# A two-layer hybrid decoder trunk: the projections behind a layer norm start on four sets of 128 columns k by k, and TensorE multiplies into an unread bank in the pause ahead of them

## The chip, the core and the metric

The kernel runs on one core of a Trainium2 chip. Its engines work in parallel, each through its own program in order, and they wait for each other through semaphores: PE (TensorE, matrix products into the eight banks of PSUM), DVE (VectorE), ACT (ScalarE), POOL (GpSimd) and SP (SyncE, which here only issues DMAs). The metric is the device time of one execution in microseconds (us).

## The reference

256 tokens and 16 learned meta tokens (272 columns in the kernel) pass through two layers. Each layer reads a normalised residual stream of 2048 features, mixes it in three ways behind one input projection, projects the result back, normalises, and applies a gated MLP of width 5632 with a causal convolution.

```python
h = _layer_norm(concatenate([meta, x], axis=1), ln_in_g, ln_in_b)
for l in range(DEPTH):                                   # DEPTH = 2
    m = _mixer(h, ...)                                   # begins with proj = h @ w_in
    h = _layer_norm(ALPHA * h + m, ln1_g[l], ln1_b[l])
    f = _conv_ffn(h, ...)
    h = _layer_norm(ALPHA * h + f, ln2_g[l], ln2_b[l])
return h[:, N_META:, :]

def _conv_ffn(h, w_up, conv_w, conv_b, w_down):
    a = h @ w_up
    ...
    val, gate = jnp.split(a, 2, axis=-1)
    return (jax.nn.silu(gate) * val) @ w_down
```

Everything is float32. There are five layer norms: n = 0 at the start, 1 and 2 in layer 0, 3 and 4 in layer 1.

## The kernel before

**Layout.** Features lie on the partitions, tokens on the free axis. `h` is the residual, 16 tiles k of 128 features by 272 tokens. A float32 product is made of three products of a shorter type (fp32r): high part of the weights times high and low part of the data, and low part of the weights times the high part of the data (L440 to L442 in `split_block`, L559 to L561 in `in_blocks`). So each tile of `h` has a high part `x_hi` and a low part `x_lo`.

**Weights.** They stream from HBM in blocks of 128 x 1024 values (512 KB) into four slots of `raw`. Of each block ACT makes the high part (`cast`, L821, into `w_hi`) and DVE the low part (`low_part`, L1154, `raw` minus `w_hi`, into `w_lo`, `in_lo_a` or `in_lo_b`). All three buffers have four slots (`SLOTS = 4`). The cast of block b waits until PE has used block b - 4 (`block_used`), and PE waits for the low part (`lo_made`, `in_lo_made`).

**A block's products.** In the up projection of the MLP a block holds 4 tiles k by 256 columns, that is two sets of 128 columns, and 24 products. Four blocks in a row (96 products) fill two banks with one group. Even groups lie in banks 0 and 1, odd ones in banks 2 and 3. In the input projection a block holds 8 tiles k by 128 columns, 24 products too; the first eight blocks are, by `IN_ORDER`, the sets 0 to 3 over k 0 to 7, and then the sets 0 to 3 over k 8 to 15, in banks 0 to 3.

**The norm.** Sums over the features are made by PE with a matrix of ones (L485 the mean, L492 the squares). Then DVE and ACT take turns. `layer_norm` on DVE: the mean's rest `shift` (L1225), its square (L1227), the variance (L1235), then `unshift` (L1231, adds `shift` to four tiles of `h`), the reciprocal of the deviation (L1241) that ACT takes the root for (L833), and a loop over eight chunks of two tiles: scaling (L1250), low part `x_lo` (L1255), with the later `unshift`s and three or four low parts of the next weights (L1154) between them at places that `late_lows` gives. `layer_norm` on ACT, for each chunk: gain and bias (L837, two instructions), then the high part `x_hi` (L842). Only behind all eight chunks does ACT go on with the cast of the fifth block (number 4).

**Behind the norms.** n = 1 and 3 stand ahead of the up projection, n = 2 (and 0) ahead of the input projection. In the up projection ACT and DVE run a loop over pairs of groups from the first group on: four casts (four low parts), then `convolve` (conv on ACT L1098 and DVE L1794, gate on ACT L1102, product on DVE L1805 to L1809). In the input projection ACT and DVE first prepare the tables of the state space: an exponential on ACT (L861), then a chain on DVE from L1446 on, with the low parts of the blocks 4 to 7 (L1154) at fixed places in it, up to `abp` (L1368), for which PE waits at its transposes (L501).

## Time and profile before

| | |
|---|---|
| time, median of 3 runs (lowest, highest) | 2651.67 us (2650.14, 2654.08) |
| the profiled execution | 2649.61 us |
| its span, first to last instruction | 2647.8 us |
| PE busy | 2529.2 us, 96% |
| DVE busy | 1784.7 us, 67% |
| ACT busy | 1370.3 us, 52% |
| TensorE's granted clock, mean | 0.979 of 2.4 GHz |

All rows name source lines as L and the number. A span of 2647.8 us with PE at 96% leaves little idle time in all; where it lies, and which engine ends it, is read from the waits and from the order in time around the norms. The five norms end near 31, 540, 1353, 1857 and 2631 us of the span.

### The profile page before, as it was taken

Reading aid. Unit: us, or ns where it says so; the run is one execution under the profiler, and the core shown is the slowest. Engines: PE = TensorE matmul, PEld = TensorE weight load, DVE = VectorE, ACT = ScalarE, POOL = GpSimd, SP = SyncE. Lnnn points to the kernel's source line nnn. Section 1 sums busy time; section 2 is a strip of 40 time slices with the busy share of each in tenths; the row PEclk is TensorE's granted clock in tenths of the full one; section 3 lists DMA queues with packets and bytes.
Section 4 is the critical chain, followed back from the end, with each engine's and each line's share of the span. In section 5 each row is a group of like instructions: output and inputs, shape, how many; then the busy total and the mean of one; then the engine's idle time right before and its main releaser. Section 6 shows DMA issues by size and latency. Waiting matters only on the chain.

```text
span 2647.8 us, 54314 instructions
## 1 busy us (share of the span) xinstructions
PE 2529.2 (96%) x21018; PEld 2414.3 (91%) x21018; DVE 1784.7 (67%) x2820; ACT 1370.3 (52%) x2131; POOL 12.2 (0%) x21
## 2 busy tenths in 40 slices
PE   5999999989999999999989999998899999999997
PEld 4999788879999999999979997888899999998886
DVE  6887577776666666545578875877766666665555
ACT  5444465465556555433354444654666556653433
POOL 0000000000000000000000000000000000000000
PEclk8999999989999999999989999999999999999998
DMA  4433232435555555555534332333455555555553
GB/s 165 152 114 129 70 113 96 136 127 169 180 173 175 168 181 173 176 172 176 174 136 158 114 132 68 112 104 128 145 181 182 183 180 177 189 183 190 184 189 114
DMA packets 109723, 401.76 MB, mean 152 GB/s; under 512 B 12176, under 2 KB 12176, under 8 KB 109584
## 3 DMA queue, kind: packets, MB, share of 16 engines
q1 hardware_dynamic: 108432, 395.15, 45.6%
q0 software_dynamic: 1152, 4.63, 0.4%
q8 instruction: 103, 1.69, 0.3%
q14 instruction: 36, 0.29, 0.0%
HBM read 397.50 MB, written 2.23 MB: 151 GB/s over the span
## 4 chain that ended last, share of the span: by engine, by line
PE 86%; DVE 9%; ACT 3%; issue 2%; DMA 1%; SPq 0%; ACTq 0%; DVEq 0%
PE ps L440 19%; PE ps L441 18%; PE ps L442 18%; PE ps L456 6%; PE ps L559 4%; PE ps L561 4%; PE ps L560 4%; PE ps L458 3%; PE ps L711 3%; PE ps L524 1%; PE ps L698 1%; DVE h L1250 1%; DVE h L1231 1%; PE ps L677 1%; PE ps L533 1%
## 5 line engine op out<-in xcount | busy, mean ns | idle before, releaser
L821 ACT ACTIVATE w_hi<-raw 128x1024 fp32r<-128x1024 f32 x728 | 764.5, 1057 | 767.4 <-PE ps L442 521.4
L1154 DVE TENSOR_TENSOR w_lo<-raw,w_hi 128x1024 fp32r<-128x1024 f32 x528 | 638.4, 1223 | 507.3 <-ACT w_hi L821 507.1
L441 PE MATMUL ps<-x_lo,w_hi 128*128 128x272 f32 (+1 forms) x2944 | 841.8, 286 | 0.0
L442 PE MATMUL ps<-x_hi,w_hi 128*128 128x272 f32 (+1 forms) x2944 | 840.4, 285 | 0.0
L440 PE MATMUL ps<-x_hi,w_lo 128*128 128x272 f32 (+1 forms) x2816 | 807.1, 287 | 20.1 <-DVE x_lo L1255 19.7
L442 PEld LDWEIGHTS ps<-x_hi,w_hi 128*128 128x128 f32 x2944 | 556.3, 189 | 0.0
L441 PEld LDWEIGHTS ps<-x_lo,w_hi 128*128 128x128 f32 x2944 | 556.3, 189 | 0.0
L440 PEld LDWEIGHTS ps<-x_hi,w_lo 128*128 128x128 f32 x2816 | 531.9, 189 | 23.2 <-issue 16.9
L561 PE MATMUL ps<-x_hi,w_hi 128*128 128x272 f32 (+1 forms) x960 | 279.7, 291 | 0.0
L560 PE MATMUL ps<-x_lo,w_hi 128*128 128x272 f32 (+1 forms) x960 | 279.6, 291 | 0.0
L456 PE MATMUL ps<-g_both,w_hi 128*128 128x512 f32 x704 | 246.4, 394 | 0.0
L440 PE MATMUL ps<-g_both,w_lo 128*128 128x272 f32 x704 | 203.3, 289 | 0.0
L441 PE MATMUL ps<-g_both,w_hi 128*128 128x272 f32 x704 | 202.5, 288 | 0.0
L442 PE MATMUL ps<-g_both,w_hi 128*128 128x272 f32 x704 | 202.1, 287 | 0.0
L458 PE MATMUL ps<-g_both,w_lo 128*128 128x256 f32 x704 | 197.1, 280 | 0.0
L560 PEld LDWEIGHTS ps<-x_lo,w_hi 128*128 128x128 f32 x960 | 185.6, 193 | 1.2
L561 PEld LDWEIGHTS ps<-x_hi,w_hi 128*128 128x128 f32 x960 | 185.5, 193 | 0.0
L559 PE MATMUL ps<-x_hi,in_lo_a 128*128 128x272 f32 (+1 forms) x480 | 149.1, 311 | 21.3 <-DVE x_lo L1255 10.8
L440 PE MATMUL ps<-y_hi,gated_w 128*128 128x272 f32 (+1 forms) x512 | 155.6, 304 | 9.2 <-DVE h L1278 7.9
L1794 DVE SCALAR_TENSOR_TENSOR conv<-ps,cpar,conv 128x271 f32<-128x271 f32 (+1 forms) x352 | 159.4, 494 | 3.1
L456 PEld LDWEIGHTS ps<-g_both,w_hi 128*128 128x128 f32 x704 | 132.3, 188 | 30.8
L442 PE MATMUL ps<-y_hi,w_hi 128*128 128x272 f32 (+1 forms) x512 | 149.1, 291 | 0.0
(287 smaller groups left out, 3827.7 us busy)
## 6 DMA issues: line engine op xcount, KB each, us to landing
raw<-stream SPq DMA_DIRECT2D x744, 512.0 KB, 3.4
h<-x SPq DMA_DIRECT2D x4, 544.0 KB, 6.3
out<-h SPq DMA_DIRECT2D x4, 544.0 KB, 2.7
cst<-consts POOLq DMA_DIRECT2D x2, 724.0 KB, 6.4
wkv<-w_kv POOLq DMA_DIRECT2D x2, 512.0 KB, 7.8
b_st<-ssm_b POOLq DMA_DIRECT2D x2, 512.0 KB, 9.2
c_st<-ssm_c POOLq DMA_DIRECT2D x2, 512.0 KB, 10.6
par<-params SPq DMA_DIRECT2D x1, 562.0 KB, 12.1
```

The costliest lines, as they stand in the source:

```text
L440: pe.matmul(acc, lo_w[:, kk, cols], hi, start=k == 0, stop=False)
L441: pe.matmul(acc, w_hi[:, slot, kk, cols], lo, start=False, stop=False)
L442: mm = pe.matmul(acc, w_hi[:, slot, kk, cols], hi, start=False, stop=k == tiles - 1)
L456: pe.matmul(ps[:, bank + j, 0:2 * n].rearrange("p (h t) -> p h t", h=2), w_hi[:, slot, kk, cols], hi_lo, start=k == 0, stop=False)
L458: mm = pe.matmul(ps[:, bank + j, 0:n], lo_w[:, kk, cols], hi_lo[:, 0, :], start=False, stop=k == tiles - 1)
L559: pe.matmul(acc, lo_w[:, kk, :], x_hi[:, k, t0:NT], start=k == 0, stop=False)
L560: pe.matmul(acc, hi_w[:, kk, :], x_lo[:, k, t0:NT], start=False, stop=False)
L561: mm = pe.matmul(acc, hi_w[:, kk, :], x_hi[:, k, t0:NT], start=False, stop=k == DT - 1)
L711: mm = pe.matmul(ps[:, 2 * (g % 2) + j, 0:NT], raw[:, n % SLOTS, kk, j * P:j * P + P], proj[:, U0 + k, :], start=k == 0, stop=k == UT - 1)
L821: act.activation(w_hi[:, slot, :, :], raw[:, slot, :, :], ACT.Copy).then_inc(hi_made, 1)
L1154: dve.tensor_tensor(w_low(phase, slot), raw[:, slot, :, :], w_hi[:, slot, :, :].bitcast(F32), ALU.subtract).then_inc(in_lo_made if phase = ...
L1794: last = dve.scalar_tensor_tensor(out=cv[:, j, tap:NT], in0=ps[:, 2 * odd + j, 0:NT - tap], scalar=cpar[:, odd, 2 + 2 * tap + j:3 + 2 * ta ...
```

## The change

1. **PE, first blocks.** `first_blocks` works through two blocks at once: for each tile k the 12 products of four sets of 128 columns. A chunk of two tiles meets 24 products in place of 12 (input projection: 6). The stream holds the first eight blocks of both projections in the order `FIRST_BLOCKS`: group 0 and 1 over k 0 to 3, group 0 and 1 over k 4 to 7, then group 0's two other blocks, then group 1's. The places are (0, 1), (2, 3), 4, 5, 6, 7; each pair waits for the low parts of both of its blocks. The loops over groups start at 1 in place of 0.
2. **PE, pause.** `idle_products` behind the sums of n = 1, 2 and 3: 10 turns of a loop of four products of a tile with itself into bank 7, which nothing reads.
3. **DVE, norm.** The first `unshift` takes two tiles in place of four, the other two come singly behind; the low part of the next block 1 stands right behind the first scaling, those of 2 and 3 further back; every `x_lo` has a place written by hand. n = 0 makes its low part 0 ahead of the reciprocal.
4. **ACT and DVE, up projection.** The first two groups stand ahead of the loop, and the first `convolve` waits for two blocks more (place 5 is the last of group 0). The input projection's first four sets are read in pairs.

```diff
+FIRST_BLOCKS = [0, 4, 1, 5, 2, 3, 6, 7]
+IDLE = 40
...
-                    it = loop.enter_context(pe.Fori(0, groups // body)) if groups > body else 0
+                    it = loop.enter_context(pe.Fori(1, groups // body)) if groups > body else 0
...
+            def first_blocks(l, phase, places, lows, t0=0):
+                sets = [(FIRST_BLOCKS[n] // KB, (first_block(l, phase) + n) % SLOTS) for n in places]
+                b = FIRST_BLOCKS[places[0]] % KB
+                pe.wait_ge(lows, first_low(l, phase) + places[-1] + 1)
+                for kk in range(KB):
+                    k = b * KB + kk
+                    if k % 2 == 0:
+                        pe.wait_ge(xlo_made, CHUNKS * (2 * l + (phase == "up")) + k // 2 + 1)
+                    for p, slot in sets:
+                        lo_w = w_low(phase, slot).rearrange("p a b -> p (a b)").rearrange("p (k m) -> p k m", k=KB)
+                        for j in range(2):
+                            acc = ps[:, 2 * p + j, t0:NT]
+                            cols = slice(j * P, j * P + P)
+                            pe.matmul(acc, lo_w[:, kk, cols], x_hi[:, k, t0:NT], start=k == 0, stop=False)
+                            pe.matmul(acc, w_hi[:, slot, kk, cols], x_lo[:, k, t0:NT], start=False, stop=False)
+                            mm = pe.matmul(acc, w_hi[:, slot, kk, cols], x_hi[:, k, t0:NT], start=False, stop=k == DT - 1)
+                        if kk == KB - 1:
+                            mm.then_inc(block_used, 1)
+            def idle_products(tile):
+                with pe.Fori(0, IDLE // 4):
+                    for _ in range(4):
+                        pe.matmul(ps[:, 7, 0:NT], tile[:, 0:P], tile, start=True, stop=True)
...
                 mm.then_inc(var_made, 1)
+                if n < 2 * DEPTH:
+                    idle_products(y_hi[:, 0, :] if n % 2 else g_hi[:, 0, :])
...
-                products(l, "up", x_parts, lambda k: (xlo_made, CHUNKS * ln + k // 2 + 1), LAST_T0[0] if l == DEPTH - 1 else 0)
+                pe.wait_ge(psum_free, first_group(l, "up") + 2)
+                for places in ((0, 1), (2, 3), (4,), (5,), (6,), (7,)):
+                    first_blocks(l, "up", places, lo_made, query_t0(l))
+                products(l, "up", x_parts, None, query_t0(l))
...
+                first = unshift(0, 1) if n else None
                 dve.wait_ge(dev_made, n + 1)
                 mark(dve.reciprocal(rstd[:, :], rstd[:, :]))
...
+                scale(0, first)
+                low_w(1)
+                if n:
+                    low_x(0)
+                    second = unshift(1, 1)
+                    scale(1, second)
+                    third = unshift(2, 2)
+                    scale(2, third)
+                    low_x(1)
+                    low_w(2)
+                    scale(3)
+                    low_x(2)
+                    fourth = unshift(4, 2)
+                    scale(4, fourth)
+                    low_w(3)
+                    low_x(3)
+                    scale(5)
+                    fifth = unshift(6, 2)
+                    low_x(4)
+                    scale(6, fifth)
+                    low_x(5)
+                    scale(7)
...
+                low_x(6)
+                low_x(7)
...
-                with act.Fori(0, FT - 2, 2) as i:
+                for e in range(2):
+                    for n in range(4):
+                        cast(l, "up", 4 * (e + 1) + n)
+                    convolve(e, e)
+                with act.Fori(2, FT - 2, 2) as i:
```

How the instructions stand on the engines. Names are those of the tiles; line numbers of the changed kernel differ.

DVE at norm n = 1, from the first `unshift` on (`h<-h,sq_out`; 128x1088 is four tiles, 128x544 two); before:

```order
L1231 TENSOR_TENSOR h<-h,sq_out 128x1088
L1241 RECIPROCAL rstd<-rstd 128x272 [waits dev_made]
L1250 TENSOR_TENSOR h<-h,rstd 128x544 [waits dve_step]
L1250 TENSOR_TENSOR h<-h,rstd 128x544
L1255 TENSOR_TENSOR x_lo<-h,x_hi 128x544 [waits xhi_made]
L1231 TENSOR_TENSOR h<-h,sq_out 128x1088
L1250 TENSOR_TENSOR h<-h,rstd 128x544 [waits dve_step]
L1154 TENSOR_TENSOR w_lo<-raw,w_hi 128x1024 [waits hi_made]
```

and in the changed kernel:

```order
L1286 TENSOR_TENSOR h<-h,sq_out 128x544
L1309 RECIPROCAL rstd<-rstd 128x272 [waits dev_made]
L1293 TENSOR_TENSOR h<-h,rstd 128x544 [waits dve_step]
L1200 TENSOR_TENSOR w_lo<-raw,w_hi 128x1024 [waits hi_made]
L1300 TENSOR_TENSOR x_lo<-h,x_hi 128x544 [waits xhi_made]
L1286 TENSOR_TENSOR h<-h,sq_out 128x544
L1293 TENSOR_TENSOR h<-h,rstd 128x544 [waits dve_step]
L1286 TENSOR_TENSOR h<-h,sq_out 128x1088
```

The shift of the second chunk is an instruction of its own now, and a weight's low part stands between the first and the second scaling.

ACT between the last high part of norm n = 1 (`x_hi<-h`) and the casts of the blocks from number 4 on (`w_hi<-raw`); before:

```order
L842 ACTIVATE x_hi<-h 128x544 [waits h_made]
L1108 UNCONDITIONAL_BRANCH
L1108 ISA
L820 REGISTER_ALU [waits w_loaded0]
L821 ACT_TABLE_LOAD
L821 ACTIVATE w_hi<-raw 128x1024 [waits block_used]
```

and in the changed kernel:

```order
L880 ACTIVATE x_hi<-h 128x544 [waits h_made]
L859 ACTIVATE w_hi<-raw 128x1024 [waits block_used,w_loaded0]
L859 ACTIVATE w_hi<-raw 128x1024 [waits block_used,w_loaded1]
L859 ACTIVATE w_hi<-raw 128x1024 [waits block_used,w_loaded2]
L859 ACTIVATE w_hi<-raw 128x1024 [waits block_used,w_loaded3]
```

The load of a table at the head of ACT's loop is gone; the changed ACT program has no table load inside that loop either, and its first one behind this place is at the first gate.

PE from the last sum of squares (`ps<-sq_out,ones_p`) to the first products of the up projection; before:

```order
L492 MATMUL ps<-sq_out,ones_p 128x272
L410 UNCONDITIONAL_BRANCH
L410 ISA
L417 ISA [waits psum_free]
L440 MATMUL ps<-x_hi,w_lo 128x272 [waits xlo_made,lo_made]
```

and in the changed kernel:

```order
L521 MATMUL ps<-sq_out,ones_p 128x272
L501 UNCONDITIONAL_BRANCH
L503 MATMUL ps<-y_hi 128x272 x4
L501 REGISTER_ALU
L501 COMPARE_AND_BRANCH
L478 MATMUL ps<-x_hi,w_lo 128x272 [waits xlo_made,lo_made,psum_free]
```

The small loop of four products stands between the sums and the wait for the first low part of the data.

## Rows read from the trace of the kernel before

**Rows 1.** Waits of PE: engine line <- releaser: total us, times, longest

```profile
PE ps L440 <- DVE x_lo L1255: 19.7, 9, 6.9
...
PE ps L501 <- DVE abp L1368: 2.9, 2, 1.5
...
PE ps L440 <- DVE w_lo L1154: 0.2, 1, 0.2
```

**Rows 2.** Timeline of PE at norm 1: start, us, instruction, idle before

```profile
546.77 0.57 PE L440 MATMUL ps<-x_hi,w_lo 128*128 128x272 f32 x1 [6.94 <-DVE x_lo L1255]
...
565.54 0.29 PE L442 MATMUL ps<-x_hi,w_hi 128*128 128x272 f32 x1
565.89 0.39 PE L440 MATMUL ps<-x_hi,w_lo 128*128 128x272 f32 x1
```

**Rows 3.** Timeline of ACT at norm 1

```profile
540.34 0.43 ACT L833 ACTIVATE rstd<-rstd 128x272 f32<-128x272 f32 x1 [5.48 <-DVE rstd L1235]
...
560.40 1.12 ACT L837 ACTIVATE h<-h,par 128x272 f32<-128x272 f32 x2 [0.59 <-DVE h L1250]
561.55 0.66 ACT L842 ACTIVATE x_hi<-h 128x544 fp32r<-128x544 f32 x1
562.22 1.28 ACT L821 ACT_TABLE_LOAD   x1
563.52 3.91 ACT L821 ACTIVATE w_hi<-raw 128x1024 fp32r<-128x1024 f32 x4
```

**Rows 4.** Timeline of DVE at norm 1

```profile
540.23 1.28 DVE L1231 TENSOR_TENSOR h<-h,sq_out 128x1088 f32<-128x1088 f32 x1
541.42 1.84 DVE L1241 RECIPROCAL rstd<-rstd 128x272 f32<-128x272 f32 x1
...
548.50 1.22 DVE L1154 TENSOR_TENSOR w_lo<-raw,w_hi 128x1024 fp32r<-128x1024 f32 x1
549.64 0.72 DVE L1250 TENSOR_TENSOR h<-h,rstd 128x544 f32<-128x544 f32 x1
550.27 0.72 DVE L1255 TENSOR_TENSOR x_lo<-h,x_hi 128x544 fp32r<-128x544 f32 x1
...
559.64 0.72 DVE L1250 TENSOR_TENSOR h<-h,rstd 128x544 f32<-128x544 f32 x1
...
564.61 4.63 DVE L1154 TENSOR_TENSOR w_lo<-raw,w_hi 128x1024 fp32r<-128x1024 f32 x4 [1.65 <-ACT w_hi L821]
```

**Rows 5.** Norm 2: last high part on ACT, head of DVE's chain, PE's wait

```profile
1373.81 0.66 ACT L842 ACTIVATE x_hi<-h 128x544 fp32r<-128x544 f32 x1
...
1376.05 0.19 DVE L1446 TENSOR_TENSOR small<-par,small 128x32 f32<-128x32 f32 x1 [0.37 <-ACT small L861]
...
1395.88 0.87 PE L501 MATMUL ps<-cst,abp 128*128 128x128 f32 x6 [1.44 <-DVE abp L1368]
```

**Rows 6.** A convolution inside the loop: its start on ACT, its last two steps on DVE

```profile
651.56 1.05 ACT L1098 ACTIVATE conv<-ps,cpar 128x272 f32<-128x272 f32 x2
...
654.99 0.44 DVE L1805 TENSOR_TENSOR prod<-gate,conv 128x272 f32<-128x272 f32 x1 [0.50 <-ACT gate L1102]
...
656.00 0.44 DVE L1809 TENSOR_TENSOR g_both<-prod,g_both 128x272 f32 x1 [0.21 <-DVE g_both L1806]
```

**Rows 7.** Stretches: us, busy (instructions) of PE, PEld, DVE, ACT, POOL, granted clock, DMA

```profile
531.50:534.20 2.70, 0.00 (x0) 0.00 (x0) 2.70 (x5) 1.06 (x1) 0.00 (x0) 1.00 0.01 3
534.20:537.60 3.40, 3.38 (x8) 2.56 (x9) 2.69 (x4) 0.66 (x1) 0.00 (x0) 0.50 0.47 154
566.00:600.00 34.00, 34.00 (x272) 34.00 (x273) 24.10 (x34) 20.91 (x28) 0.00 (x0) 1.00 0.62 198
1849.90:1853.20 3.30, 0.20 (x2) 0.00 (x0) 3.20 (x6) 1.18 (x3) 0.00 (x0) 1.00 0.00 0
1853.20:1856.60 3.40, 3.40 (x14) 2.62 (x15) 3.12 (x6) 0.64 (x1) 0.00 (x0) 1.00 0.48 154
1810.80:1817.60 6.80, 6.03 (x28) 6.03 (x29) 5.25 (x7) 0.53 (x2) 0.00 (x0) 0.50 0.55 188
```

More of the change, by code:

```diff
@@ L420, in products @@
                             else:
-                                split_block(phase, slot, b, 2 * (g % 2), blocks * KB, rhs, ready if g == 0 else None, t0)
+                                split_block(phase, slot, b, 2 * (g % 2), blocks * KB, rhs, ready if ready and g == 0 else None, t0)
                         if phase != "up" and g == 2:
@@ L1236, in layer_norm, with unshift, scale, low_x @@
                                              op0=ALU.mult, op1=ALU.subtract).then_inc(spread_made, 1)
-                    unshifted = [unshift(0)]
                 else:
                     first_norm_stats()
+                    low_part(*low_parts, 0)
+                def unshift(c, chunks):
+                    part = h[:, 2 * c:2 * (c + chunks), :]
+                    return mark(dve.tensor_tensor(part, part, spread(shift, 2 * chunks), ALU.add))
+                def scale(c, shifted=None):
+                    if shifted:
+                        after(shifted)
+                    h2 = h[:, 2 * c:2 * c + 2, :]
+                    dve.tensor_tensor(h2, h2, spread(rstd[:, :], 2), ALU.mult).then_inc(scaled, 1)
+                def low_x(c):
+                    if n < 2 * DEPTH:
+                        dve.wait_ge(xhi_made, CHUNKS * n + c + 1)
+                        t = slice(2 * c, 2 * c + 2)
+                        dve.tensor_tensor(x_lo[:, t, :], h[:, t, :], x_hi[:, t, :].bitcast(F32), ALU.subtract).then_inc(xlo_made, 1)
+                def low_w(b):
+                    if low_parts:
+                        low_part(*low_parts, b)
+                first = unshift(0, 1) if n else None
                 dve.wait_ge(dev_made, n + 1)
@@ L1242, in layer_norm @@
                 after()
-                late_lows = (1, 4, 5, 6) if n == 0 else (2, 4, 6) if n % 2 else (4, 6, 7)
-                for c in range(CHUNKS + 2):
-                    if c < CHUNKS:
-                        if n and c % 2 == 0:
-                            after(unshifted[c // 2])
-                        h2 = h[:, 2 * c:2 * c + 2, :]
-                        dve.tensor_tensor(h2, h2, spread(rstd[:, :], 2), ALU.mult).then_inc(scaled, 1)
-                    if (c == 1 or c >= 3) and n < 2 * DEPTH:
-                        part = max(c - 2, 0)
-                        dve.wait_ge(xhi_made, CHUNKS * n + part + 1)
-                        t = slice(2 * part, 2 * part + 2)
-                        dve.tensor_tensor(x_lo[:, t, :], h[:, t, :], x_hi[:, t, :].bitcast(F32),
-                                          ALU.subtract).then_inc(xlo_made, 1)
-                    if n and c in (1, 3, 5):
-                        unshifted.append(unshift(c // 2 + 1))
-                    if low_parts and c in late_lows:
-                        low_part(*low_parts, 4 - len(late_lows) + late_lows.index(c))
+                scale(0, first)
@@ new lines, in layer_norm @@
+                low_w(1)
[19 more added lines that the diff above has]
+                    scale(7)
+                else:
+                    scale(1)
+                    low_x(0)
+                    scale(2)
+                    low_x(1)
+                    low_w(2)
+                    scale(3)
+                    low_x(2)
+                    scale(4)
+                    low_w(3)
+                    low_x(3)
+                    scale(5)
+                    low_x(4)
+                    scale(6)
+                    low_x(5)
+                    scale(7)
@@ L1809, in convolve @@
                     dve.tensor_tensor(lo, pr_, hi.bitcast(F32), ALU.subtract).then_inc(g_made, 1)
-                with dve.Fori(0, FT - 2, 2) as i:
+                for e in range(2):
+                    for n in range(4):
+                        low_part(l, "up", 4 * (e + 1) + n)
+                    convolve(e, e)
+                with dve.Fori(2, FT - 2, 2) as i:
                     for e in range(2):
```

37 lines of the change are left out of this document (23 added, 14 removed).

## The prediction

> **What bounds the kernel now.** I read the waits of PE first, since PE is busy for 96% of the span. Its largest group is the wait for `x_lo` at the norms: 19.7 us in the up projections, of it 6.9 us at once [rows 1]. That looks like the prize of this change: more products for each chunk of data, and no cold start. But idle time ahead of a stage is worth something only if the wait that ends last in the stage moves. So I read the timelines in order.
>
> At norm 1 PE starts its products at 546.77 and issues the last of the first group at 565.54; the fifth block's first product follows at 565.89 [rows 2]. The wait there is only 0.2 us, for `w_lo` [rows 1], so two chains end at almost the same moment: PE's 96 products, and the fifth block's low part. The second chain is this: ACT makes the last `x_hi` at 561.55, loads a table at 562.22, casts block 4 at 563.52 [rows 3]; DVE makes its low part at 564.61 [rows 4]; PE starts 1.28 us behind that. With four slots PE can't do more than 96 products before that moment, in whatever order they come. From 566 on it is busy without a gap at the full clock, 272 products in 34.00 us [rows 7], so what is won or lost at 565.89 is carried to the end.
>
> At norm 2 the last wait is another: PE waits for `abp` at its transposes until 1395.88, 1.44 us idle, and `abp` ends DVE's chain that started at 1376.05, released by ACT behind its last `x_hi` at 1373.81 [rows 5]. Norm 0 has the same shape.
>
> So the question is not how fast PE gets through the first chunks, but when ACT's last `x_hi` is made.
>
> **The change part by part.**
>
> *The norm on DVE, n = 1.* Distances from start to start: 0.64 us for two tiles (549.64 to 550.27), 1.14 for a low part of weights (548.50 to 549.64) [rows 4]; a shift that the next instruction needs costs its full length and 0.04, so 1.32 for four tiles and 0.76 for two. The first shift of two tiles takes 0.64, and ACT's root ends at 540.77 [rows 3], so the reciprocal starts at 540.87 in place of 541.42 [rows 4]: 0.55 us early. The first scaling starts 1.84 + 0.04 later, at 542.75. From there to the last scaling the new order holds 13 steps of 0.64 (seven scalings, six `x_lo`), three low parts of 1.14, shifts of 0.76 + 1.32 + 1.32 + 1.20, and one wait of 0.82 for the first `x_hi` (0.76 + 1.15 [rows 3] + 0.69 behind the scaling, less 1.78 of work done meanwhile): 8.32 + 3.42 + 4.60 + 0.82 = 17.16, so it starts at 559.91. Before it was 559.64 [rows 4]. ACT needs 1.71 us a chunk (1.15 from gain to `x_hi` [rows 3], then 0.56, the 0.66 of the `x_hi` less its overlap with the next) and gets the last two scalings only 1.28 apart, so its last `x_hi` starts at 558.63 + 0.76 + 1.71 + 1.15 = 562.25, against 561.55: **0.70 us later**.
>
> *The table.* Before, the casts behind the norm stand at the head of a loop and a table is loaded there: 1.30 us from 562.22 to 563.52 [rows 3]. The changed program has none at this place. The cast starts 0.56 behind the `x_hi`, at 562.81, the low part 1.09 later at 563.90, PE 1.28 later at 565.18: **0.71 us earlier** than 565.89. The Trainium skill (ScalarE: Activation LUTs, What ACT_TABLE_LOAD costs) prices a change of table at 1.28 us for the load and 1.38 for a drain, 2.66 in all; the row has 1.28 and the next cast right behind it, so it shows no drain here. By the page each up projection would gain 1.4 us more, and the sum below would be 2.7 us lower.
>
> *k by k.* The first product comes at 546.24 (0.55 early). Chunk 0 gives 24 products x 0.125 = 3.0 us, to 549.2; chunk 1 has its `x_lo` at 550.1 and ends at 553.2; the second pair waits for low part 3, which DVE ends at 555.6, so chunk 2 ends at 558.8 and chunk 3 at 561.8. All 96 products are then done, and PE stands still for **3.4 us** until 565.18. The weave gains nothing: it moves the pause from ahead of the chunks to ahead of block 4.
>
> *What that pause costs.* Pauses of this length have gone both ways. Behind one of 2.7 us the granted clock was 0.50 (1.2 GHz) for the next 3.4 us; behind one of 3.3 us it stayed at 1.00; once the low stretch was 6.8 us long [rows 7]. At the low level 28 products took 6.03 us, 0.215 each, where 0.12 is usual: 0.45 us lost for each us. Here nothing hides it, since PE is the bound from block 4 on. A low stretch of 3.4 us costs 1.5 us, none costs 0, one of 6.8 costs 3.0. I take 1.5 for each up projection: the pause will be longer than 2.7 us, and at norm 3 it is 3.8 us, since the 258 columns there make PE faster.
>
> *Idle products.* 40 x 0.125 = 5.0 us behind the sums, inside a pause of 6.9 us [rows 1]. If a turn of the loop costs nothing beside its products they end 1.4 us ahead of the first chunk and keep the clock up for it. That is worth nothing, because the time at which block 4 starts doesn't hang on it. Bounds: 0, and, if the turns are slow, still 0 up to 3.4 us of delay.
>
> *First convolution.* It may start when group 0 is complete, T. With the start on ACT as 0, the product's last step comes at 4.44 (651.56 to 656.00 [rows 6]), the low part of block 8 0.36 behind it, its end 1.22 later, PE 0.06 later: 6.1, and 0.2 from T to the start. PE needs it when places 6 and 7 are done, 6.0 us behind T (5.76 at norm 3). A new wait of **0.3 and 0.5 us**.
>
> *Norm 2.* The same 17.16 us of DVE, but before, the third low part stood behind the last scaling. With the first scaling at 1356.15 the same steps put the last `x_hi` at 1375.65, against 1373.81 [rows 5]: 1.84 us later. The table for the exponential is still loaded there. The whole chain to `abp` shifts by that, and PE's wait with it: **+1.84 us**. PE itself isn't late: block 4 can start at 1382.0, and even with 6.8 us at the low clock its four blocks end at 1397.1, ahead of 1397.7.
>
> *Norms 0 and 4.* At n = 0 low part 0 goes into DVE's idle time ahead of the reciprocal; by the same steps ACT ends 0.3 us earlier. At n = 4 the reciprocal is 0.55 early, the extra shift costs 0.76: +0.2.
>
> *Sum.* -0.3 (n = 0) + (-0.71 + 0.3 + 1.5) + 1.84 + (-0.71 + 0.5 + 1.5) + 0.2 = **+4.1 us**. On the profiled execution (span 2647.8, time 2649.6) that gives 2653.7; the median of the runs is 2.06 above it, so 2651.7 + 4.1 = **2655.8 us**. Bounds of the sum: +1.1 with no fall of the clock, +7.1 with the long ones.
>
> **The rivals.**
>
> A. *The clock holds in both pauses.* For it speaks the pause of 3.3 us behind which it stayed at 1.00, against it the one of 2.7 us [rows 7]. The rest stays: +1.1, **2652.8 us**.
>
> B. *Slower: the pause ahead of block 4 brings a low stretch of 6.8 us in both up projections.* PE's work for the chunks is pressed together, then it stands still 3.4 and 3.8 us, and starts cold where it is the bound. For it speaks the stretch of 6.8 us [rows 7]. It counts as slower once the two stretches lose 4.2 us together. +1.1 + 2 x 3.0 = +7.1, **2658.8 us**. The Trainium skill (TensorE: Matmul & The Clock Gate, HAM oscillation) describes just this: groups of products shorter than the wait between them leave the engine cold for each next group. The rows agree for one pause and disagree for another.
>
> C. *Faster, as the change is meant.* If block 4 could start when the 96 products are done, 561.8 in place of 565.9, each up projection would gain 4.1 us: with -0.3, +1.84 and +0.2 that is -6.5, **2645.2 us**. Against it stand the order of casts on ACT and the four slots; it needs a chain behind the last `x_hi` that is 3.4 us shorter than I worked out.
>
> D. *The idle loop doesn't do what it says.* If a turn takes 1.4 us in place of 0.5, the loop ends at 554 and the 96 products, 12.0 us, at 566; the pause is filled with late work, the clock holds, and each up projection starts block 4 some 0.8 us later than in A: +2.7, **2654.4 us**. No row shows so short a loop on PE.
>
> **How the numbers follow.** Forecast 0.45, A 0.20, B 0.18, C 0.06, D 0.05, others 0.06 (half of them faster). The range takes in A, D, the forecast and B's centre with a run's own spread of some 2 us (2650.1 to 2654.1 before): 2650.5 to 2660. What a measurement of this kernel can tell from no change is about 0.2%, 5.3 us: slower begins at 2657.0. Slower holds B and the upper part of the forecast (one long and one short stretch, +5.6): 0.32. Faster: C and half of the others: 0.09. Within: 0.59.
>
> **What the changed profile would show.** The first product at norm 1 some 0.5 us earlier behind the sums, and a granted clock of 1.00 in the stretch of the chunks where it was 0.50. A wait of PE for `w_lo` of 3 to 4 us ahead of block 4, twice, where it was 0.2. No table load between the last `x_hi` and the cast, and PE's restart 2.93 us behind that `x_hi`'s start, in place of 4.34. At norm 2 the last `x_hi` 1.8 us later, measured from the sums of squares, and PE's wait at the transposes longer. After the restart a stretch at 0.50. I am wrong if the last `x_hi` is not later at norms 1 and 2, if PE has no pause ahead of block 4, or if a stall that these rows don't hold shows up, such as an engine slowed by PE's extra reads.

## The result, and the profile after

| | before | changed kernel |
|---|---|---|
| median of 13 runs each (lowest, highest) | 2650.14 us (2647.42, 2654.36) | 2656.69 us (2652.47, 2659.67) |
| ratio to before, 95% interval | | 1.0019 [1.0012, 1.0026] |
| the profiled execution, its span | 2649.61, 2647.8 us | 2656.88, 2655.1 us |
| PE, DVE, ACT busy | 2529.2, 1784.7, 1370.3 us | 2544.8, 1784.3, 1269.5 us |

The change costs about 0.2%, 3 to 7 us by the interval. The forecast was 2655.8, +4.1 us. Its starting point was the median of three runs, 2651.67, which lies 1.5 us above the median of 13 here.

**Waits of PE** in the changed kernel (columns as in [rows 1]):

```profile
PE ps L478 <- DVE x_lo L1300: 12.1, 7, 5.8
PE ps L478 <- DVE w_lo L1200: 9.7, 4, 3.4
```

The prize that [rows 1] seemed to offer was collected: of the 19.7 us for `x_lo` in the up projections alone, 12.1 are left over all norms, in good part because 5 us of idle products now fill each pause (25.0 without them, in experiment 1). In its place stand waits for low parts of weights, 9.7 us where there were 0.2, and the time is no better. The pause has moved from ahead of the chunks to ahead of block 4.

**ACT and DVE at norm 1**, timelines (start, us, instruction, idle before), for [rows 3] and [rows 4]:

```profile
563.95 0.66 ACT L880 ACTIVATE x_hi<-h 128x544 fp32r<-128x544 f32 x1
564.51 2.94 ACT L859 ACTIVATE w_hi<-raw 128x1024 fp32r<-128x1024 f32 x3
...
565.59 2.36 DVE L1200 TENSOR_TENSOR w_lo<-raw,w_hi 128x1024 fp32r<-128x1024 f32 x2 [0.22 <-ACT w_hi L859]
```

**PE at norm 1**, for [rows 2]: the sums' last products, the idle products, the first product of the first pair of sets, of its second chunk, of the second pair, the last of the 96, block 4.

```profile
540.70 0.85 PE L521 MATMUL ps<-sq_out,ones_p 128*128 128x272 f32 x3
541.19 5.38 PE L503 MATMUL ps<-y_hi 128*128 128x272 f32 x40
547.94 0.36 PE L478 MATMUL ps<-x_hi,w_lo 128*128 128x272 f32 x1 [1.38 <-DVE x_lo L1300]
...
551.86 0.39 PE L478 MATMUL ps<-x_hi,w_lo 128*128 128x272 f32 x1 [0.67 <-DVE x_lo L1300]
...
557.37 0.60 PE L478 MATMUL ps<-x_hi,w_lo 128*128 128x272 f32 x1 [2.22 <-DVE w_lo L1200]
557.76 0.43 PE L479 MATMUL ps<-x_lo,w_hi 128*128 128x272 f32 x1
...
564.82 0.29 PE L480 MATMUL ps<-x_hi,w_hi 128*128 128x272 f32 x1
566.87 0.39 PE L478 MATMUL ps<-x_hi,w_lo 128*128 128x272 f32 x1 [1.76 <-DVE w_lo L1200]
```

The first row merges three products of the sums, of which the last starts at 541.16. The 40 idle products take 5.4 us and end ahead of the first chunk. No table is loaded between `x_hi` and the cast, and PE restarts 2.92 us behind that `x_hi` (4.34 before). But the `x_hi` itself is later, and PE, which has worked off the 96 products at 564.82, stands still for 2 us. At norm 3 the pause is longer, and the clock behind it is low from the first product:

```profile
1884.62 0.28 PE L480 MATMUL ps<-x_hi,w_hi 128*128 128x258 f32 x1
1888.34 0.53 PE L478 MATMUL ps<-x_hi,w_lo 128*128 128x258 f32 x1 [3.44 <-DVE w_lo L1200]
1888.67 0.42 PE L479 MATMUL ps<-x_lo,w_hi 128*128 128x258 f32 x1
```

**Stretches** of the changed kernel (columns as in [rows 7]): the idle products; the first low stretch, inside the woven products; the one behind the restart at norm 1; the one behind the restart at norm 3; and the stretch that follows at norm 1.

```profile
541.20:547.90 6.70, 5.37 (x42) 5.11 (x40) 5.53 (x7) 2.21 (x4) 0.00 (x0) 1.00 0.08 12
557.30:560.70 3.40, 3.33 (x15) 3.33 (x16) 3.40 (x6) 2.47 (x5) 0.00 (x0) 0.51 0.50 158
567.50:570.90 3.40, 3.40 (x18) 3.40 (x17) 2.72 (x3) 1.00 (x2) 0.00 (x0) 0.50 0.77 234
...
1888.40:1891.80 3.40, 3.40 (x16) 3.40 (x17) 3.29 (x3) 1.56 (x3) 0.00 (x0) 0.50 0.75 201
...
571.00:605.00 34.00, 33.96 (x271) 33.73 (x270) 21.77 (x32) 16.82 (x23) 0.00 (x0) 1.00 0.57 190
```

In 3.40 us at the low level PE starts 16 and 18 products; at the full one, with 0.125 us each, it would be 27. So 9 to 11 products are missing, 1.1 to 1.4 us. Nothing is given back later: 34 us hold 272 products before [rows 7] and 271 after.

**Norm 2**, for [rows 5]: the last high part, the head of DVE's chain, PE's wait.

```profile
1378.46 0.66 ACT L880 ACTIVATE x_hi<-h 128x544 fp32r<-128x544 f32 x1
1379.14 1.28 ACT L899 ACT_TABLE_LOAD   x1
...
1380.69 0.19 DVE L1536 TENSOR_TENSOR small<-par,small 128x32 f32<-128x32 f32 x1 [0.81 <-ACT small L899]
...
1400.52 1.09 PE L532 MATMUL ps<-cst,abp 128*128 128x128 f32 x8 [1.06 <-DVE abp L1458]
```

**Distances.** Absolute times of two executions can't be compared stage by stage, because the start of a stage carries what happened ahead of it. So all timelines are read from the same place: z is the start of the last product of a norm's sums (at norm 1 539.44 before, 541.16 after; at norm 2 1352.84 and 1355.68; at norm 3 1856.93 and 1862.65). In us, one profiled execution of each kernel:

| | before | after | no idle products | norm only | loops only | table back | casts early | scalings first | both | early, no weave |
|---|---|---|---|---|---|---|---|---|---|---|
| norm 1: z to first product | 7.34 | 6.78 | 6.77 | 6.77 | 7.34 | 6.78 | 6.78 | 6.78 | 6.78 | 7.34 |
| z to last `x_hi` | 22.11 | 22.79 | 22.76 | 22.76 | 22.11 | 22.77 | 23.89 | 22.77 | 23.91 | 22.41 |
| z to last of 96 products | 26.10 | 23.66 | 22.18 | 25.71 | 26.10 | 22.19 | 23.61 | 22.19 | 22.21 | 26.64 |
| z to block 4 | 26.45 | 25.71 | 25.68 | 27.10 | 26.22 | 27.20 | 23.73 | 25.69 | 22.35 | 26.76 |
| norm 1 to norm 2 | 813.41 | 814.52 | 814.42 | 814.06 | 813.08 | 816.88 | 810.90 | 814.46 | 809.61 | 813.62 |
| norm 2: z to last `x_hi` | 20.97 | 22.78 | 22.77 | 22.76 | 20.98 | 22.77 | 22.76 | 18.92 | 18.92 | 20.98 |
| z to PE's transposes | 43.03 | 44.84 | 44.82 | 44.83 | 43.05 | 44.82 | 44.82 | 41.53 | 41.52 | 43.06 |
| norm 3: z to last of 96 | 25.94 | 21.97 | 23.44 | 25.66 | 25.94 | 23.44 | 21.98 | 23.44 | 23.44 | 26.60 |
| z to block 4 | 26.46 | 25.69 | 25.68 | 27.11 | 26.06 | 27.20 | 22.35 | 25.68 | 23.56 | 26.73 |
| norm 3 to norm 4 | 773.25 | 774.56 | 774.53 | 773.90 | 772.74 | 775.90 | 769.71 | 774.53 | 770.82 | 773.40 |

The columns behind the second are experiments 1 to 8 below, in their order. The rows "norm 1 to norm 2" and "norm 3 to norm 4" run from z to z and hold the MLP.

### The profile page after: what moved, and what is told of

Same layout as the page of the kernel before. It is cut to its first block, busy times and chain, and to the rows that moved or that the text cites. A ratio compares the mean times of both kernels' runs of the same rounds, so it can differ in the third digit from the quotient of the medians.

```text
span 2655.1 us, 54291 instructions
## 1 busy us (share of the span) xinstructions
PE 2544.8 (96%) x21138; PEld 2431.2 (92%) x21138; DVE 1784.3 (67%) x2824; ACT 1269.5 (48%) x2049; POOL 12.2 (0%) x21
## 4 chain that ended last, share of the span: by engine, by line
PE 86%; DVE 8%; ACT 3%; issue 2%; DMA 1%; SPq 0%; ACTq 0%; DVEq 0%
PE ps L443 18%; PE ps L444 18%; PE ps L445 18%; PE ps L459 6%; PE ps L594 4%; PE ps L596 4%; PE ps L595 4%; PE ps L461 3%; PE ps L746 2%; PE ps L555 1%; PE ps L733 1%; DVE h L1293 1%; DVE h L1286 1%; PE ps L564 1%; PE ps L712 1%
## 5 line engine op out<-in xcount | busy, mean ns | idle before, releaser
L444 PE MATMUL ps<-x_lo,w_hi 128*128 128x272 f32 (+1 forms) x2816 | 802.8, 285 | 0.0
L445 PE MATMUL ps<-x_hi,w_hi 128*128 128x272 f32 (+1 forms) x2816 | 801.5, 285 | 0.0
L443 PE MATMUL ps<-x_hi,w_lo 128*128 128x272 f32 (+1 forms) x2688 | 766.7, 285 | 0.3 <-DVE w_lo L1200 0.3
L445 PEld LDWEIGHTS ps<-x_hi,w_hi 128*128 128x128 f32 x2816 | 529.8, 188 | 0.0
L444 PEld LDWEIGHTS ps<-x_lo,w_hi 128*128 128x128 f32 x2816 | 529.6, 188 | 0.0
L443 PEld LDWEIGHTS ps<-x_hi,w_lo 128*128 128x128 f32 x2688 | 505.3, 188 | 0.8 <-DVE w_lo L1200 0.8
L596 PE MATMUL ps<-x_hi,w_hi 128*128 128x272 f32 (+1 forms) x832 | 240.1, 289 | 0.0
L595 PE MATMUL ps<-x_lo,w_hi 128*128 128x272 f32 (+1 forms) x832 | 240.0, 289 | 0.0
L459 PEld LDWEIGHTS ps<-g_both,w_hi 128*128 128x128 f32 x704 | 132.3, 188 | 30.8
L595 PEld LDWEIGHTS ps<-x_lo,w_hi 128*128 128x128 f32 x832 | 158.7, 191 | 1.2
L596 PEld LDWEIGHTS ps<-x_hi,w_hi 128*128 128x128 f32 x832 | 158.5, 191 | 0.0
L444 PEld LDWEIGHTS ps<-g_both,w_hi 128*128 128x128 f32 x704 | 132.4, 188 | 0.0
```

Source lines behind the costliest of these rows:

```text
L443: pe.matmul(acc, lo_w[:, kk, cols], hi, start=k == 0, stop=False)
L444: pe.matmul(acc, w_hi[:, slot, kk, cols], lo, start=False, stop=False)
L445: mm = pe.matmul(acc, w_hi[:, slot, kk, cols], hi, start=False, stop=k == tiles - 1)
L459: pe.matmul(ps[:, bank + j, 0:2 * n].rearrange("p (h t) -> p h t", h=2), w_hi[:, slot, kk, cols], hi_lo, start=k == 0, stop=False)
L595: pe.matmul(acc, hi_w[:, kk, :], x_lo[:, k, t0:NT], start=False, stop=False)
L596: mm = pe.matmul(acc, hi_w[:, kk, :], x_hi[:, k, t0:NT], start=False, stop=k == DT - 1)
```

## The experiments

Ratios are to the kernel before, run on the same chip beside each group: its median was 2652.06 us with experiments 1 to 4, 2652.55 with 5 to 8, and 2651.53 with the two of 9.

**1. Without the idle products.** The changed kernel less

```diff
-                if n < 2 * DEPTH:
-                    idle_products(y_hi[:, 0, :] if n % 2 else g_hi[:, 0, :])
```

> The changed kernel without its idle products, all else as it is. Theory (the fifth block's low part ends the stage, whatever PE did before): the first chunks run at the low clock, chunk 0 takes 5.4 us in place of 3.0, yet the 96 products are still done 2 to 4 us ahead of block 4; from the last sum of squares to block 4's first product 25.7 us at norms 1 and 3, as in the changed kernel (25.71, 25.69), and to the transposes at norm 2 44.8 us as there (44.84). Time equal to the changed kernel's within the clock's scatter of 2 us. Rival (the idle products earn a part of the time): those distances grow, by up to 2.4 us a norm, and the kernel is some 5 us slower than the changed one.

Measured: 2657.26 us, ratio 1.0027 [1.0017, 1.0037]. Its stretches and its first product at norm 1:

```profile
539.00:543.90 4.90, 0.24 (x2) 0.00 (x0) 4.59 (x5) 1.42 (x3) 0.00 (x0) 1.00 0.00 0
543.90:550.80 6.90, 5.17 (x23) 5.21 (x24) 6.09 (x9) 4.35 (x8) 0.00 (x0) 0.51 0.21 76
```

```profile
545.62 0.57 PE L478 MATMUL ps<-x_hi,w_lo 128*128 128x272 f32 x1 [6.38 <-DVE x_lo L1298]
```

The first chunk is now multiplied at the low level, 23 products in the 6.9 us. Nothing comes of it: the last `x_hi`, block 4, and the whole up projection lie within 0.1 us of the changed kernel. The idle products do hold the clock up, and the clock held up is worth nothing there, since PE waits for each chunk anyway. Nor did they save the clock at the pause that matters: with and without them it is low behind block 4 in both up projections.

**2. The norm's new order alone.** The kernel before with DVE's `layer_norm` of the changed one, from `first = unshift(0, 1)` to `low_x(7)` in the change's diff:

```diff
-                late_lows = (1, 4, 5, 6) if n == 0 else (2, 4, 6) if n % 2 else (4, 6, 7)
-                for c in range(CHUNKS + 2):
...
+                scale(0, first)
+                low_w(1)
+                if n:
+                    low_x(0)
+                    second = unshift(1, 1)
...
```

> The kernel before with nothing but VectorE's new order in the norms. Theory (the last x_hi decides): from the last sum of squares to the last x_hi 22.8 us at norm 1 and 3 (22.11 before) and 22.8 at norm 2 (20.97); block 4 starts at 27.1 at norms 1 and 3 (26.45), since the table load is still there, and the transposes at norm 2 at 44.8 (43.03). Sum -0.2 + 0.7 + 1.8 + 0.7 + 0.2 = +3.2 us on the kernel before. Rival (the order of VectorE is neutral and the weave or its cold restart makes the loss): distances as before and a time as before.

Measured: 2656.33 us, ratio 1.0016 [1.0007, 1.0026]. The last `x_hi` comes 0.65 and 1.79 us later at norms 1 and 2, block 4 0.65 us later, the transposes 1.80 us later. With norms 0 and 4 (-0.3 and +0.2) these distances add up to +3.0 us, where the changed kernel's terms give +4.3. So most of the loss is made by the norm's order, with no woven product in the program.

**3. The loops alone.** The kernel before, with the first two groups ahead of the loop on ACT and the same on DVE:

```diff
-                with act.Fori(0, FT - 2, 2) as i:
+                for e in range(2):
+                    for n in range(4):
+                        cast(l, "up", 4 * (e + 1) + n)
+                    convolve(e, e)
+                with act.Fori(2, FT - 2, 2) as i:
```

> The kernel before with the first two groups of ScalarE and VectorE taken ahead of their loops, so that no table load stands ahead of block 4's cast. Theory (two chains end together there): the low part of block 4 comes 1.3 us earlier, but PE's own 96 products end as before at 26.1 us behind the last sum of squares, so block 4 starts at 26.2 in place of 26.45 and the kernel gains 0.2 us in each up projection: no change that can be measured. Rival (the table load is worth its full 1.3 us in each): -2.6 us, block 4 at 25.1.

Measured: 2651.3 us, ratio 0.9998 [0.9989, 1.0008]. Block 4 comes 0.23 and 0.40 us earlier, not 1.3: the 96 products end at 26.10 and 25.94 as before, and PE has no more to gain than the little wait that there was. The up projections are 0.33 and 0.51 us shorter, too little for the runs to tell from nothing.

**4. The table back.** The changed kernel, with one small activation that needs the table, ahead of block 4's cast:

```diff
+                act.activation(gate[:, 0, 0:8], par[:, 0:8], ACT.Silu)
                 for e in range(2):
                     for n in range(4):
                         cast(l, "up", 4 * (e + 1) + n)
```

> The changed kernel with one small Silu on ScalarE (128 x 8) ahead of block 4's cast, which puts the table load back in its place (the later one at the first gate goes). Theory: block 4 starts later by the load and the small instruction, 1.3 + 0.2 = 1.5 us, at 27.2 us behind the last sum of squares at norms 1 and 3 (25.7 now), and the kernel is 3 us slower than the changed one. By the Trainium skill's price of a table change (2.66 us) it would be 2.9 us at each and 5.7 in all. Rival (PE is late there for another reason): no shift.

Measured: 2661.24 us, ratio 1.004 [1.0026, 1.0054]. ACT and PE at norm 1:

```profile
561.95 0.66 ACT L880 ACTIVATE x_hi<-h 128x544 fp32r<-128x544 f32 x1
562.62 1.28 ACT L1150 ACT_TABLE_LOAD   x1
563.91 0.21 ACT L1150 ACTIVATE gate<-par 128x8 f32<-128x8 f32 x1
564.03 1.99 ACT L859 ACTIVATE w_hi<-raw 128x1024 fp32r<-128x1024 f32 x2
```

```profile
561.37 0.29 PE L480 MATMUL ps<-x_hi,w_hi 128*128 128x272 f32 x1
566.38 0.59 PE L478 MATMUL ps<-x_hi,w_lo 128*128 128x272 f32 x1 [4.72 <-DVE w_lo L1201]
```

From the start of `x_hi` to that of the cast it is 2.08 us in place of 0.56, and block 4 is 1.49 and 1.51 us later. Here, where the cast sets the restart, a table costs its length, and behind the longer pause more: the first up projection is 2.36 us longer than in the changed kernel, 0.87 beyond the shift of block 4, and the low stretch was 6.8 us long (565.0 to 571.7 in the trace) in place of 3.4. At norm 3 the low stretch was 3.4 us as in the changed kernel, and the loss 1.34. The two up projections together are 3.70 us longer than in the changed kernel, where 3 were expected. From the start of the load to the start of the next activation it is 1.29 us, so the drain that the Trainium skill adds to the load (ScalarE: Activation LUTs, What ACT_TABLE_LOAD costs) isn't seen here either.

These four say where the loss comes from. They also say what would have to move: the cast of block 4, which stands behind all eight copies, although PE has used its slot once the first pair of sets is through. The next kernels try that.

**5. The casts early.** The changed kernel, with the casts of blocks 4 and 5 between ACT's chunks and their low parts ahead of DVE's last two `x_lo` (the part ahead of the loops then begins with block 6; not shown):

```diff
@@ ACT, layer_norm, in the loop over chunks c @@
                         act.activation(x_hi[:, 2 * c:2 * c + 2, :], h[:, 2 * c:2 * c + 2, :], ACT.Copy).then_inc(xhi_made, 1)
+                        if early is not None and c in (5, 6):
+                            cast(early, "up", c - 1)
@@ DVE, layer_norm @@
+                if n % 2:
+                    low_w(4)
                 low_x(6)
+                if n % 2:
+                    low_w(5)
                 low_x(7)
```

> The changed kernel, with ScalarE's casts of the up projections' blocks 4 and 5 moved inside the norm, behind the copies of chunks 5 and 6, and VectorE's low parts of the same two blocks ahead of the last two x_lo. My theory: in the changed kernel block 4 comes late only because its cast stands behind all eight copies; the four woven sets end about 22.2 us behind the last product of the sums when the clock is high, and block 4 can then start at once. So the restart moves from 25.7 us to about 22.3 us behind that product, at both up projections, and with no pause the clock has nothing to fall for: 3.3 us for the pause and up to 1.5 us for the clock, each. Against the changed kernel the up stages of layer 0 and 1 (last product of one norm's sums to that of the next) are 3.3 to 4.8 us shorter, the whole 7 to 9.6 us, near 2648. Norm 2 stays as it is, 44.8 us from its sums to the next landmark. Rival: the work merely moves, since VectorE or ScalarE is full there, the last x_hi comes 1 us later and the up stages gain under 1.5 us each; near 2655.

Measured: 2649.11 us, ratio 0.9992 [0.9983, 1.0001]. The up projections are 3.62 and 4.85 us shorter than in the changed kernel (3.3 to 4.8 expected), though the last `x_hi` is 1.1 us later, as the rival had it: that no longer matters, because block 4 doesn't wait for it. Block 4 starts 0.12 and 0.37 us behind the last of the 96 products. One number was missed: 22.3 us came at norm 3 only, at norm 1 it was 23.7. There a low stretch fell among the woven products, as in the changed kernel.

**6. The scalings first at norm 2.** The changed kernel; at even n DVE's order becomes

```diff
+                if n and n % 2 == 0:
+                    second = unshift(1, 1)
+                    low_x(0)
+                    scale(1, second)
+                    third = unshift(2, 2)
+                    scale(2, third)
+                    scale(3)
+                    low_x(1)
+                    fourth = unshift(4, 2)
+                    scale(4, fourth)
+                    scale(5)
+                    low_x(2)
+                    fifth = unshift(6, 2)
+                    scale(6, fifth)
+                    scale(7)
+                    low_w(2)
+                    low_w(3)
+                    low_x(3)
+                    low_x(4)
+                    low_x(5)
```

> The changed kernel, with VectorE's order at norm 2 (and 4) changed alone: the shifts and scalings run ahead, with two x_lo between them, and the low parts of weight blocks 2 and 3 and the other x_lo behind the last scaling. My theory: the path through norm 2 runs over the last scaling to ScalarE's last copy and from there to the end of the in projection's first tiles, so each us that the last scaling comes earlier is gained until TensorE's own products are what is late. Last copy at norm 2 about 3 us earlier (22.8 to about 19.7 us behind the last product of the sums), the landmark behind the first projection tiles from 44.8 to about 41.6 us, which is 1.4 us better than in the kernel before (43.0). Whole 3 us less than the changed kernel, near 2654. Rival: TensorE's products at norm 2 then wait for the low parts of blocks 2 and 3 and for x_lo, and the landmark stays within 1 us of 44.8.

Measured: 2653.1 us, ratio 1.0003 [0.9993, 1.0012]. The last `x_hi` at norm 2 comes 3.86 us earlier, more than the 3 expected, and PE's transposes 3.31 us earlier:

```profile
1395.17 1.09 PE L532 MATMUL ps<-cst,abp 128*128 128x128 f32 x8 [1.47 <-DVE abp L1478]
```

PE still waits for `abp` there, 1.47 us, so its own products weren't late even in this order.

**7. Both edits,** those of experiments 5 and 6, in one kernel.

> Both edits together, the casts moved inside the norm ahead of the up projections and the scalings first at norm 2. The stages are far apart and share nothing, so the gains add: 7 to 9.6 us plus 3.2 us against the changed kernel. About 2645 (2642 to 2648), 5 to 8 us (0.2 to 0.3%) under the kernel before. Restart at 22.3 us behind the sums at both up projections, 41.6 us at norm 2. If instead the loss against the kernel before were spread over other stages, these two local gains would show in the distances and not in the whole time.

Measured: 2645.35 us, ratio 0.9974 [0.9965, 0.9983]. PE at norm 1:

```profile
561.18 0.29 PE L480 MATMUL ps<-x_hi,w_hi 128*128 128x272 f32 x1
561.32 0.39 PE L478 MATMUL ps<-x_hi,w_lo 128*128 128x272 f32 x1
```

There is no pause between the 96 products and block 4, and it starts 4.1 us earlier than in the kernel before (22.35 against 26.45 us behind z). Against the kernel before, the first up projection is 3.80 us shorter, norm 2 1.51, the second up projection 2.43. Its ratio lies below 1 and below that of the changed kernel, so this version is faster than both, by 0.26% than the kernel before.

**8. The casts early without the weave.** The kernel of experiment 3, with the early casts on ACT as in experiment 5, and on DVE, whose order in the norm is that of the kernel before:

```diff
+                    if n % 2 and c >= CHUNKS:
+                        low_part(*low_parts, c - 4)
                     if (c == 1 or c >= 3) and n < 2 * DEPTH:
```

> The kernel before with no woven sets and its own order in the norm, only the two first convolution groups ahead of the loops and the casts and low parts of blocks 4 and 5 moved inside the norm as in the run beside it. It tells whether the weave is what makes the moved casts worth something. My theory: in the kernel before the first 96 products themselves end only 26.1 us behind the sums, since the second pair of sets waits for nothing but TensorE, so block 4 that is ready at 22 us meets a busy engine: restart stays at 26.1 us, the up stages within 0.5 us of those with the loops unrolled alone (813.1 and 772.7 us), near 2651. Rival: the order of TensorE doesn't matter and the early cast gives the same 3.3 us here, near 2645.

Measured: 2651.45 us, ratio 1.0001 [0.9992, 1.0011]. No gain, as expected: block 4 meets an engine that is busy with the 96 products. They even end 0.54 and 0.66 us later than in experiment 3, which I had not counted. On DVE the two low parts, 1.14 us each, now stand ahead of the last `x_lo`:

```profile
563.01 1.22 DVE L1160 TENSOR_TENSOR w_lo<-raw,w_hi 128x1024 fp32r<-128x1024 f32 x1
564.15 0.72 DVE L1263 TENSOR_TENSOR x_lo<-h,x_hi 128x544 fp32r<-128x544 f32 x1
```

So the weave needs the early cast, and the early cast needs the weave; each alone is worth nothing or less. (No run has the weave with the old order of the norm; that the weave alone gains nothing is seen from the changed kernel, where block 4 waits for its low part with the 96 products done.)

**9. Both edits without the idle products,** and experiment 7 once more beside it.

> The kernel with both edits (casts of blocks 4 and 5 inside the norm, scalings first at norm 2), without the 40 products ahead of the first woven set. In the changed kernel these were worth nothing, but there ScalarE's cast set the restart; here TensorE's own 96 products set it, so that it could matter now whether the clock is high when they begin. My theory: still nothing. The first six chunks arrive one by one and TensorE waits for each, so the low clock is used up on waiting; the 96 products end at 22.2 or 23.5 us behind the sums as in the run with the 40 products, restart 22.3 or 23.7, norm 2 at 41.5, all within 0.2 us of one of these, the whole near 2645. Rival: without them the clock stays low until a later chunk and the 96 products end about 1.5 us later than either, 25 us, at both up projections, the whole near 2648.5.

> The kernel with both edits once more, unchanged, beside the one without the 40 products and on the same chip as it, for the comparison of the two and a second measure of the gain: ratio to the kernel before 0.9965 to 0.9983 as in the first measurement.

Measured: 2645.46 us, ratio 0.9976 [0.9967, 0.9985] without them, and 2645.97 us, 0.9979 [0.997, 0.9988] with them. All distances of the two up projections agree within 0.02 us (block 4 at 22.32 and 23.58 us without, 22.33 and 23.58 with). Without the idle products PE worked from 547.2 to 554.0 at the low level:

```profile
547.20:554.00 6.80, 5.11 (x22) 5.14 (x23) 6.00 (x9) 4.31 (x8) 0.00 (x0) 0.50 0.25 77
```

and the 96 products ended at the same distance. The idle products can be left out.

## Why the prediction was right, point by point

| term of the sum | predicted | measured |
|---|---|---|
| norm 0 (start of the span to the first transposes, 70.95 to 70.78) | -0.3 | -0.17 |
| first up projection (norm 1 to norm 2) | +1.1 | +1.11 |
| norm 2 | +1.84 | +1.81 |
| second up projection (norm 3 to norm 4) | +1.3 | +1.31 |
| norm 4 (to the end, 17.65 to 17.86) | +0.2 | +0.21 |
| sum | +4.1 | +4.27 |

**The last `x_hi`** was predicted 0.70 us later at norm 1 and 1.84 at norm 2, and came 0.68 and 1.81 later. Counting the steps of DVE between the first and the last scaling was what the prediction rested on, and experiment 2 shows that the norm's order alone makes the larger part of the loss.

**The table.** Block 4 0.71 us earlier was forecast, 0.74 and 0.77 it was. Experiments 3 and 4 split this: worth 1.5 us in the changed kernel, 0.2 and 0.4 in the kernel before.

**The pause and the clock.** The forecast had 3.4 and 3.8 us of pause and a low stretch of 3.4 us behind each. Measured from the last product's start the pauses were 2.05 and 3.72, and each was followed by 3.4 us at half speed. From block 4 to the product 96 further on, the first up projection took 13.88 us in place of 12.13: 1.75, of it 0.2 for the wait for the first convolution, which leaves 1.5 for the clock. In the second it was 13.60 in place of 11.63: 1.97, with 0.5 for that wait, and again 1.5 for the clock. At norm 1 the term came out right although its reason didn't hold: 1.5 was taken because the pause would be longer than 2.7 us, and it was shorter. That the clock fell there all the same was luck for the forecast. The shorter pause of norm 1 has its cause in a place where I had expected none: behind the pause of 2.5 us ahead of the second pair of sets the clock fell too, and the 96 products ended 1.3 us later than worked out (23.66 behind z for 22.36). It cost nothing, as block 4 wasn't there yet. In experiments 1, 4, 6 and 7 this stretch didn't come at norm 1, and they end at 22.2, but it came at norm 3. The weave gained nothing, as said: C, the change as it was meant, asked for block 4 at the end of the 96 products, and experiments 5 and 7 show what was missing for it.

**The first convolution.** 0.3 and 0.5 us were forecast. The rows of the changed kernel have block 8 0.34 us behind the last product of place 7, where 0.13 is the usual distance, so 0.2:

```profile
580.41 0.29 PE L480 MATMUL ps<-x_hi,w_hi 128*128 128x272 f32 x1
580.75 0.39 PE L443 MATMUL ps<-x_hi,w_lo 128*128 128x272 f32 x1
```

At norm 3 the same gap was 0.59, so 0.46.

**Norm 2.** That PE would not be late there holds further than I had need of. In the changed kernel it had a pause of 5.5 us and 6.8 us at the low level behind it (1383.3 to 1390.1), in experiment 2 the clock was low for 17.1 us from 1357.2 on, as in the kernel before (from 1356.8); the transposes came at 44.84 and 44.83 us. One sign that was forecast didn't come: PE's wait at the transposes was to be longer, and it was 1.06 us for 1.44 before, because PE's own four blocks end 2.2 us later behind z than before (the last product starts at 43.50 for 41.31), while `abp` comes 1.8 later. So PE has less slack there than before.

**The idle products** were predicted to be worth nothing and to take 5.0 us beside the work; both hold (5.4). The first chunk's product came 0.56 us earlier for 0.55.

**The rivals.** Of no low stretch (A), 6.8 us in both (B) and the value between, this execution had the one between, 3.4 us twice. B's mechanism exists: experiment 4 lengthens the pause and gets it once. The four profiled kernels that pause longest ahead of block 4 (the changed one and experiments 1, 4 and 6) have eight such pauses, of 2.05 to 5.0 us from the last product's start. The clock was low at or just behind the restart in all eight, for 3.4 us in seven and for 6.8 in one; behind the two pauses of 1.4 us in experiment 2 it wasn't. That speaks against A, but A can't be excluded for other executions of the changed kernel, whose times go from 2652.47 to 2659.67. D, a slow loop, is out.

**The rest of the profile.** The profiled executions differ by 7.3 us of span, the terms by 4.27. The other 3.0 lie between the first transposes and norm 1 (+1.91) and between those of layer 1 and norm 3 (+1.07), where the change touches nothing. One pair of profiled executions can't charge them to it, because as much comes and goes with the same program: experiment 7 and its repeat are the same program, their distances agree within 0.1 us in the up projections, norm 2 and the end, and the stage from the first transposes to norm 1 took 468.56 us in one and 471.54 in the other. Both had a pause of PE of 1.4 us in the attention; then the clock was low for 3.4 us in the first and for 10.2 us in the second. The windows, the first two of experiment 7, the others of its repeat:

```profile
298.40:301.80 3.40, 3.20 (x7) 2.50 (x8) 0.81 (x3) 0.64 (x4) 0.00 (x0) 0.50 0.00 0
301.80:308.60 6.80, 6.80 (x36) 4.37 (x35) 2.14 (x6) 1.75 (x7) 0.00 (x0) 1.00 0.22 81
```

```profile
297.90:301.30 3.40, 2.77 (x6) 2.19 (x7) 0.81 (x3) 1.07 (x5) 0.00 (x0) 0.50 0.00 0
301.30:308.10 6.80, 6.80 (x17) 3.76 (x15) 1.19 (x3) 1.03 (x3) 0.00 (x0) 0.50 0.01 2
```

Over the twelve profiled executions this stage took 468.5 to 471.6 us and the one of layer 1 461.1 to 465.3. But neither is it shown that these 3.0 us are no part of the price: the eight executions with woven sets average 469.7 and 464.1 us in these two stages, the four without 468.8 and 462.1. The terms' sum, +4.27, is 1.0016 of the time, within the ratio's interval. The whole moved by about 5.0 us by the ratio and by 6.55 by the two medians. So the terms are well forecast, but that the forecast 2655.8 is only 0.9 us from the median 2656.69 owes something to luck: the starting point was 1.5 us too high, and that made up for part of what the sum lacks. What isn't settled is what decides whether such a stretch is short or long.

## What to carry to other kernels

Before giving an idle engine more to do at the head of a stage, find what releases the first piece of work that it can't have done by then; if that is a step at the end of another engine's list, reorder the work only together with that step. Here the weave and the early cast gained nothing or lost when each was alone. Together they shortened the two up projections by 2.5 and 3.5 us against the kernel before (experiment 5), and with the scalings first at norm 2 the whole kernel by 0.2 to 0.3% (experiment 7). When a reordering adds small instructions to the engine that paces a norm, count its steps to the last one that others wait for: that count gave the delay of the last `x_hi` to 0.1 us, and distances from a landmark in the same stage verify it where whole executions scatter by more.

## What the runs showed of the hardware that was not expected

The same pause behind the same work has both outcomes. In the changed kernel and in experiment 7, PE runs 48 products of the first pair of sets at the full clock, stands still for 2.5 us, and goes on with the second pair; once it is at half speed, once at the full clock. Windows of the changed kernel (the stretch behind its pause is the second row of its stretches, 0.51), then of experiment 7:

```profile
547.90:555.00 7.10, 6.39 (x48) 6.13 (x48) 7.03 (x9) 4.92 (x9) 0.00 (x0) 1.00 0.30 96
```

```profile
545.70:552.70 7.00, 6.28 (x48) 6.09 (x48) 6.93 (x9) 4.82 (x9) 0.00 (x0) 1.00 0.28 99
555.00:558.40 3.40, 3.23 (x25) 3.23 (x26) 3.40 (x6) 2.74 (x6) 0.00 (x0) 1.00 0.47 154
```

Within experiments 5 and 7 the fall sits at norm 1 in one and at norm 3 in the other (block 4 at 23.73 and 22.35 us, and at 22.35 and 23.56), so the pair of up projections loses it once either way.

A loop of four products a turn on PE cost little beside the products: 40 of them took 5.4 us, where 0.125 us for each would be 5.0.

The Trainium skill (TensorE: Matmul & The Clock Gate, HAM oscillation) warns of groups of products shorter than the waits between them. The trace agrees only in part: the clock was low behind block 4's pause in both up projections of the changed kernel, but the groups here aren't shorter than the waits. The 96 products ahead of block 4 take 17 and 15 us from the first to the last, the pauses 2.05 and 3.72. So the prediction went too far when it said that the page describes just this case. The trace adds where a low clock costs time: the 6.9 us of low clock in the chunks of experiment 1 cost nothing, the 3.4 us behind block 4 cost 1.5.
